# Stick-breaking attention: paired value products, key blocks summed on GpSimd, a reordered TensorE program and a fourth logit buffer

## What is computed

```python
def sb_block(q, k, v, bias, q_pos, k_pos):
    z = jnp.einsum('bqhd,bkhd->bhqk', q, k) * (SB_HEAD_DIM ** -0.5) + bias[None, :, None, None]
    causal = (k_pos[None, :] < q_pos[:, None])[None, None]
    log_stay = jnp.where(causal, jax.nn.log_sigmoid(-z), 0.0)
    between = lax.cumsum(log_stay, axis=3, reverse=True) - log_stay
    weight = jnp.where(causal, jnp.exp(jax.nn.log_sigmoid(z) + between), 0.0)
    return jnp.einsum('bhqk,bkhd->bqhd', weight, v)
```

## Time and profile before

| | us |
|---|---|
| median of 3 runs | 1560.82 |
| lowest and highest run | 1552.71, 1561.26 |
| the profiled execution | 1563.84 |
| its span, first to last instruction | 1561.6 |
| the attention, from the scores of head 0 to the last copy of sample results | 172.64 to 290.52 |

### The profile page before, as it was taken

One profiled execution on the slowest core, in us unless ns is written; L12 is line 12 of the kernel. 1 busy time (PEld: TensorE's weight loads), 2 busy tenths in 40 slices (PEclk: granted clock), 3 DMA queues, 4 the chain that ended last, 5 costly groups with the idle time before them and its releaser, 6 DMA issues. The chain is left out here.

```text
span 1561.6 us, 16192 instructions
## 1 busy us (share of the span) xinstructions
PE 1371.1 (88%) x6197; PEld 1072.5 (69%) x6198; DVE 1038.4 (66%) x1081; ACT 691.2 (44%) x667; POOL 241.2 (15%) x224
## 2 busy tenths in 40 slices
PE   2899899996599989998879999897589999999893
PEld 2786355686478868887758884486568878887672
DVE  3278844214698878885854999523578888886753
ACT  2010344002467867873530007221347777775532
POOL 1033222001112322220000000001102233321000
PEclk6899899996699999999989999998579999999896
DMA  7457536007279999996460302012259999995301
GB/s 268 167 196 302 196 109 241 28 1 264 92 276 371 313 360 373 370 355 234 133 215 1 108 14 99 0 52 59 68 177 372 388 309 382 389 372 221 113 1 55
DMA packets 122739, 314.04 MB, mean 201 GB/s; under 512 B 10060, under 2 KB 10720, under 8 KB 120608
## 3 DMA queue, kind: packets, MB, share of 16 engines
q1 hardware_dynamic: 106350, 249.82, 44.4%
q0 software_dynamic: 14256, 58.69, 10.3%
q10 hardware_dynamic: 2074, 4.71, 1.1%
HBM read 304.17 MB, written 26.70 MB: 212 GB/s over the span
## 5 line engine op out<-in xcount | busy, mean ns | idle before, releaser
L1694 PE MATMUL ps<-xnT,ring 128*128 128x260 f32 x1408 | 318.5, 390 | 13.0 <-DVE xnT L1188 7.0
L1694 PEld LDWEIGHTS ps<-xnT,ring 128*128 128x128 f32 x1408 | 273.2, 194 | 57.9 <-issue 14.4
L1916 PE MATMUL ps<-ring_parts,arena_parts 128*128 128x512 f32 x768 | 308.9, 402 | 0.0
L1448 DVE TENSOR_TENSOR ring_parts<-ring,xnT_parts 128x2048 fp32r<-128x2048 f32 x96 | 219.3, 2291 | 47.8 <-ACT xnT_parts L967 46.8
L1448 DVE TENSOR_TENSOR ring_parts<-ring,arena_parts 128x2048 fp32r<-128x2048 f32 x96 | 219.7, 2291 | 40.2 <-ACT arena_parts L967 39.7
L967 ACT ACTIVATE xnT_parts<-ring 128x2048 fp32r<-128x2048 f32 x96 | 183.4, 1917 | 87.6 <-PE ps L1917 76.4
L967 ACT ACTIVATE arena_parts<-ring 128x2048 fp32r<-128x2048 f32 x96 | 183.5, 1918 | 75.5 <-PE ps L1917 53.1
L1916 PEld LDWEIGHTS ps<-ring_parts,arena_parts 128*128 128x128 f32 x768 | 148.5, 193 | 32.4
L1915 PE MATMUL ps<-xnT_parts,arena_parts 128*128 128x512 f32 x384 | 158.7, 413 | 10.1 <-DVE arena_parts L1452 10.1
L1915 PE MATMUL ps<-arena_parts 128*128 128x512 f32 x384 | 156.4, 407 | 8.4 <-DVE arena_parts L1452 4.7
L1917 PE MATMUL ps<-xnT_parts,arena_parts 128*128 128x512 f32 x384 | 155.1, 404 | 0.0
(11 more groups left out here) (274 smaller groups left out, 1734.6 us busy)
## 6 DMA issues: line engine op xcount, KB each, us to landing
ring<-in_w_gate_e SPq DMA_DIRECT2D x32, 2048.0 KB, 17.5
ring<-in_w_up_e SPq DMA_DIRECT2D x32, 2048.0 KB, 16.7
ring<-in_w_down_e SPq DMA_DIRECT2D x32, 2048.0 KB, 18.4
ring<-in_w_in_ab SPq DMA_DIRECT2D x4, 2048.0 KB, 26.1
ring<-in_w_ple_gate SPq DMA_DIRECT2D x4, 2048.0 KB, 8.1
ring<-y_rows SPq DMA_DIRECT2D x16, 512.0 KB, 7.1
ring<-in_w_in_c SPq DMA_DIRECT2D x4, 2048.0 KB, 8.9
x_rows<-arena ACTq DMA_DIRECT2D x10, 416.0 KB
```

What stands on the lines that cost most here:

```text
L1448: v.tensor_tensor(w_lo, w, high[hu0 % 4].bitcast(F32), ALU.subtract).then_inc(s_lo, 1)
L1694: ins = mm(s[:, half, 0:HALF], w[:, k, :], src[:, k, half * HALF:(half + 1) * HALF], start=(k == 0), stop=(k == n - 1))
L1916: mm(ps[:, bank, :], x, w_lo, start=False, stop=False)
```

## The change

Four things change, all in the attention.

1. GpSimd masks the softplus of head h before the weights of head h-1, no longer after them. It then adds key blocks up into a spare area: two copies of 128 columns, one addition of 128 and one of 384 columns, with two waits on its own results. `sticks` then needs one `ones` product in place of up to three for each key block: seven products, 2048 columns, instead of ten and 2560.
2. `values(p)` takes two heads at a time, key block by key block, and stands in even rounds only, behind the scores of head h+1 and the sample values, and in front of the sticks of head h. It waits for the masked weights of both heads.
3. Sample values and `turn_sample` come one round later; the sample values stand right behind the scores.
4. There are four logit buffers; the fourth lies over queries and keys that have been used by then. Which head takes which, and which value products it waits for, stands in two tuples.

```diff
+LOGIT_BUF = (0, 1, 2, 0, 1, 3, 2, 0)
+LOGIT_FREE = (0, 0, 0, 2, 2, 0, 4, 4)
...
             for h in range(SBH):
+                pool.wait_ge(s_sp, h + 1)
+                sp, later = ex[:, h % 2, :], spare[h % 2]
+                link(mask(sp))
+                pool.tensor_copy(later[:, 0:P], sp[:, 1024:1024 + P])
+                pool.tensor_copy(later[:, 256:256 + P], sp[:, 512:512 + P])
+                link(pool.tensor_tensor(later[:, P:256], sp[:, 1024 + P:1280], sp[:, 896:1024], ALU.add))
+                pool.tensor_tensor(later[:, 256 + P:640], sp[:, 512 + P:896], later[:, 0:256], ALU.add
+                                   ).then_inc(s_spm, 1)
                 if h:
                     mask_weights(h - 1)
-                pool.wait_ge(s_sp, h + 1)
-                mask(ex[:, h % 2, :]).then_inc(s_spm, 1)
...
                 act.wait_ge(s_zf, h + 1)
-                if h >= 3:
-                    act.wait_ge(s_pv, h - 2)
+                if LOGIT_FREE[h]:
+                    act.wait_ge(s_pv, LOGIT_FREE[h])
...
                 if h:
                     pe.wait_ge(s_dd, h)
-                if h >= 2:
-                    turn_sample(h - 2)
+                if h >= 3:
+                    turn_sample(h - 3)
                 pe.wait_ge(s_spm, h + 1)
-                sp = ex[:, h % 2, :]
+                sp, later = ex[:, h % 2, :], spare[h % 2]
+                behind = (later[:, 256:640], later[:, 0:256], sp[:, 896:1024])
                 for kb in range(4):
-                    for src in range(kb, 4):
...
+                    col, width = c0 + at[kb], TP - kb * P
+                    ins = mm(ps_flat[:, col:col + width], tri[:], sp[:, at[kb]:at[kb] + width],
+                             start=True, stop=(kb == 3), skip_group_check=True)
+                    if kb < 3:
+                        ins = mm(ps_flat[:, col + P:col + width], ones[:], behind[kb],
+                                 start=False, stop=True, skip_group_check=True)
                 ins.then_inc(s_cf, 1)
...
+            def values(p):
+                pe.wait_ge(s_wm, 2 * p + 2)
+                if p:
+                    pe.wait_ge(s_ot, p)
                 for kb in range(4):
+                    for h in (2 * p, 2 * p + 1):
+                        rows = slice(64 * (h % 2), 64 * (h % 2) + 64)
+                        ins = mm(ps[rows, 6, kb * P:TP], v_tok[:, kb, h * DH:(h + 1) * DH],
+                                 zs3[LOGIT_BUF[h]][:, at[kb]:at[kb] + TP - kb * P], start=(kb == 0), stop=(kb == 3),
+                                 skip_group_check=True)
+                ins.then_inc(s_pv, 2)
...
             for h in range(SBH):
                 if h + 1 < SBH:
                     scores(h + 1)
-                if h:
-                    values(h - 1)
+                if h >= 2:
+                    sample_values(h - 2)
+                    if h % 2 == 0:
+                        values(h // 2 - 1)
                 sticks(h)
...
+            sample_values(SBH - 2)
+            pe.wait_ge(s_dd, SBH)
+            turn_sample(SBH - 3)
             sample_values(SBH - 1)
-            values(SBH - 1)
-            pe.wait_ge(s_dd, SBH)
             turn_sample(SBH - 2)
+            values(SBH // 2 - 1)
             turn_sample(SBH - 1)
```

More of the change, by code:

```diff
@@ L247, in decoder_step @@
         ar = Arena()
-        qT = ar(4, T)
-        kT = ar(4, T)
+        qk = ar(4, 2, T)
+        qT, kT = qk[:, :, 0, :], qk[:, :, 1, :]
         v_tok = ar(NRT, 512)
@@ L254, in decoder_step @@
         ex = ar(2, 1280)
-        zs3 = [zs[:, 0, :], zs[:, 1, :], xnT[:, 4:KT, :].rearrange("p k t -> p (k t)")[:, 0:1280]]
+        zs3 = [zs[:, 0, :], zs[:, 1, :], xnT[:, 4:KT, :].rearrange("p k t -> p (k t)")[:, 0:1280],
+               arena[:, 0:1280]]
+        spare = [xnT[:].rearrange("p k t -> p (k t)")[:, 3360:4000], sq[:].rearrange("p a b -> p (a b)")[:, 0:640]]
         ar = Arena(spans)
@@ L714, in mask_weights @@
                 pool.wait_ge(s_we, h + 1)
-                mask(zs3[h % 3]).then_inc(s_wm, 1)
+                mask(zs3[LOGIT_BUF[h]]).then_inc(s_wm, 1)
             for h in range(SBH):
+                pool.wait_ge(s_sp, h + 1)
[6 more added lines that the diff above has]
+                                   ).then_inc(s_spm, 1)
                 if h:
                     mask_weights(h - 1)
-                pool.wait_ge(s_sp, h + 1)
-                mask(ex[:, h % 2, :]).then_inc(s_spm, 1)
                 if h < 2:
@@ L910, in weights @@
                 act.wait_ge(s_dd, h + 1)
-                nc.scalar.activation(zs3[h % 3], zs3[h % 3], ACT.Exp).then_inc(s_we, 1)
+                nc.scalar.activation(zs3[LOGIT_BUF[h]], zs3[LOGIT_BUF[h]], ACT.Exp).then_inc(s_we, 1)
             for h in range(SBH):
-                zb, eb = zs3[h % 3], ex[:, h % 2, :]
+                zb, eb = zs3[LOGIT_BUF[h]], ex[:, h % 2, :]
                 act.wait_ge(s_zf, h + 1)
-                if h >= 3:
-                    act.wait_ge(s_pv, h - 2)
+                if LOGIT_FREE[h]:
+                    act.wait_ge(s_pv, LOGIT_FREE[h])
                 nc.scalar.activation(zb, z, ACT.Identity, bias=sbb[:, h:h + 1], scale=DH ** -0.5).then_inc(s_zs, 1)
@@ L1305, in attend_back @@
             def attend_back(h):
-                zb = zs3[h % 3]
+                zb = zs3[LOGIT_BUF[h]]
                 dve.wait_ge(s_cf, h + 1)
@@ L1797, in sticks @@
-                ins.then_inc(s_cf, 1)
[L1799 to L1803, removed]
-                for kb in range(4):
[L1805 to L1808, removed]
+                    col, width = c0 + at[kb], TP - kb * P
@@ L1841, in _ @@
                        ).then_inc(s_cs, 1)
-                else:
-                    sample_values(h - 1)
+            sample_values(SBH - 2)
+            pe.wait_ge(s_dd, SBH)
+            turn_sample(SBH - 3)
             sample_values(SBH - 1)
-            values(SBH - 1)
-            pe.wait_ge(s_dd, SBH)
             turn_sample(SBH - 2)
+            values(SBH // 2 - 1)
             turn_sample(SBH - 1)
```

## The result

| | before | after |
|---|---|---|
| median of 13 runs each, us | 1554.39 | 1542.61 |
| lowest and highest run | 1548.19, 1561.26 | 1535.19, 1549.3 |
| ratio of times, 95% interval | | 0.9921 [0.9899, 0.9943] |
| span of the profiled execution | 1561.6 | 1538.3 |
| the attention stage, as in front | 117.88 (172.64 to 290.52) | 105.29 (171.09 to 276.38) |

The change made the kernel 12 us faster, 0.8%. That is within the 1% that the forecast called no change, but the time, 1542.61, lies 3.4 us under the low end of the range. Two things went into the miss. The 13 runs of the kernel before have a median 6.4 us lower than the three of them that the forecast started from. And the gain was 12 us where 7.4 was forecast: 0.9921 measured, 1553.4 / 1560.8 = 0.9953 forecast, just outside the interval. The second alone would have stayed in the range, at 1560.8 - 12.5 = 1548.3.

The account below looks back on a forecast made before the run. TensorE was taken to set the pace in the attention's middle rounds, not the first ones or round 7. A walked gain of 12.5 us less 5.1 for the clock gave 7.4: 1560.8 to 1553.4 us, range 1546 to 1562.

Parts of the forecast that it names:

- the 1% that the forecast called no change: Whole kernel: 15.6 us counted as indistinguishable; chances 0.85 within 1%, 0.10 faster, 0.05 slower.
- The walk: Attention stage: new order followed instruction by instruction with the old trace's durations; 12.5 us gained before any clock loss.
- the clock term: TensorE idling ahead of three pairs of values: half clock behind each, 3 x 1.7 = 5.1 us lost, ends 0 and 6.6.
- twice the select's 0.83 on 0.185: GpSimd's additions before sticks: twice a select's rate per column, 0.82 us for 384 columns and 0.40 for 128.
- nothing ahead of sticks 2 comes later than before: Start of attention: softplus of head 2 still ends at 204.49, so sticks 2 start at 211.0, 3.6 us gained.
- the clock stays full: Rival, attention: TensorE's stalls cost no clock, so 12.5 us gained, 1548.3 us; chance 0.17.
- both old stalls: Earlier trace, TensorE ahead of values: stalls of 2.14 and 3.06 us, followed by losses of 1.7 and 2.2 us.
- The ceiling: Attention: TensorE's shorter sticks and paired values would give 16 us, 1.0%, if TensorE stayed the pace.
- the 2.27 of the rival: Rival, values: the two heads' products don't run side by side, 2.27 us more four times, 1562.5 us; chance 0.05.
- GpSimd was not late: Rival, ahead of three pairs: dear additions or waits for VectorE, some 2 us a pair, 1559.4 us; chance 0.13.
- Half clock up to the end of the next sticks: Rival, three pairs: values, turned sample and sticks, 6.85 us, take twice that, 8 us slower, 1568.9 us; chance 0.08.
- round 7 (7.1 us): Last attention round: values go behind, leaving 6.4 us of 13.46 between sticks 6 and sticks 7 ends; 7.1 us gained.

Follow-up runs that it names:

- sticks first: Changed kernel with pairs of values behind the sticks of their round and four logit buffers in turn; 1538.19 us (0.9874) and 1535.92 us (0.9877).
- the filled one: Changed kernel with four logit buffers in turn, plus four unneeded products ahead of each of the first three pairs of values; 1543.18 us (0.9913).
- the one with heads in blocks: Changed kernel with a pair's value products issued all for the first head, then all for the second, not alternating; 1547.52 us (0.9936).
- The fourth buffer: Changed kernel with the four logit buffers taken in turn, so head 3 need not wait for the first pair; 1541.58 us (0.9922) and 1535.36 us.
- The triple mask: Changed kernel with GpSimd's mask of the weights run three times instead of once, same data; 1558.12 us (1.0034).
- The first last-round edit: Kernel before with values of head 6 moved behind sticks of head 7, in round 7 alone; 1557.52 us (1.0021).
- the second 1.7 less: Kernel before with values of head 6 behind sticks 7 and GpSimd masking the softplus before the previous head's weights; 1558.04 us, one run.

## Why the prediction was right or wrong

**The walk held.** Starts of sticks in us from the start of the stage, without the clock term. The walked ones come from the prediction's 211.0 for sticks 2 and its durations from there on, less 172.64:

| | walked | measured |
|---|---|---|
| sticks 2 | 38.4 | 38.7 |
| sticks 4 | 62.8 | 62.8 |
| sticks 6 | 85.2 | 84.8 |
| sticks 7 | 91.6 | 91.2 |
| last copy | 105.4 | 105.3 |

12.5 us were walked and 12.6 measured. Its prices were close. Sticks took 3.65 us (3.61 taken), a pair 2.37 (2.33, for which the prediction gives no working; the rate of the earlier trace rows alone would make it 1.94 x 2560 / 2048 = 2.43). GpSimd's sums took 1.8 us, from 227.83 to 229.65 (2.0 taken, bounds 1.6 and 2.5). The difference is in the 384-column addition, 0.73 us where 0.82 was taken, and in the two waits, 0.07 and 0.08 (0.16 each). The form of the addition's price was wrong: from 0.45 us for 128 columns and 0.73 for 384 it is 1.1 ns a column on some 0.31 us, not twice the select's 0.83 on 0.185. The two errors cancel at these sizes, which is luck.

The walk took it that nothing ahead of sticks 2 comes later than before, and there it was 0.6 us off: the softplus of head 2 ended 32.5 us behind the stage's start, 31.9 before. In round 0 VectorE's seven additions ran beside GpSimd's new sums and took 2.53 us instead of 1.83 (the kernel before first, then the change); without the sums they took 1.83 again. The faster sums made up for a third of it.

```profile
185.74 1.83 DVE L1276 TENSOR_TENSOR arena<-arena 128x64 f32<-128x64 f32 x7
184.17 2.53 DVE L1286 TENSOR_TENSOR arena<-arena 128x64 f32<-128x64 f32 x7
```

Of the other kernels, the first with sticks first and the filled one came within 0.3 us of their walks, and the one without sums within 1. The one with heads in blocks came within 0.5 by luck: 2.3 us a pair were expected at full clock, and it paid 1.55 a pair and the rest in half clock. The others missed. The fourth buffer took 3.4 and 1.7 us more than walked and the second execution of sticks first 1.9, each with half clock on the chain. The triple mask took 9.0 more, by the lock with VectorE and by half clock. The first last-round edit took 1.9 more (115.8 expected, 117.72 measured), because its walk left GpSimd's order out, and the second 1.7 less.

**The clock term failed.** "I take 3 x 1.7 = 5.1" is the step. It made one stall of 2.14 us a price for every stall of that length. In three profiles of the change none of nine stalls ahead of values, six of 1.06 to 1.61 us and three of 2.18 to 2.21, was followed by half clock. The rival "the clock stays full" is what happened behind these stalls: 12.5 us, a ratio of 1548.3 / 1560.8 = 0.9920, against 0.9921 measured. I gave it 0.17 because "both old stalls" spoke against it. The experiments show what that evidence was worth. Of the stalls ahead of values in all profiles, the kernel before among them, all eight of 2.74 us and more lost the clock. Of ten between 2.14 and 2.41 us three did and seven did not. Length alone does not decide: the shorter stalls ahead of sticks 1, 1.80 to 1.95 us in the three profiles of the change, were all followed by half clock. The prediction kept 0 as an end of the clock term, but put its weight on the other side. The stalls were also shorter than it said (1.06 us instead of 3.0, 2.18 instead of 2.6). Most of the first difference is the half-clock stretch in sticks 3, which took up 1.7 us of that stall.

**The starting point.** The forecast went down from 1560.8, and 13 runs put the kernel before at 1554.39. With that and the walk alone, 1554.4 - 12.5 = 1541.9, 0.7 us under the time measured, closer than the interval (some 3.4 us either way) can tell. The range allowed for full clock and for a median 3 us off; the median was 6.4 off, and that took the time below the range.

**The ceiling and the other rivals.** TensorE spared 16 us of work was named as a ceiling only, and that is right: without the sums the stage loses 3.3 us, not 7.2. The products do run side by side; in blocks a pair takes 1.55 us more, not the 2.27 of the rival. GpSimd was not late ahead of the three pairs: its masks there took 1.02 or 1.03 us, and no addition was dear. Beside VectorE it was slowed in round 0 alone, where its mask took 1.43 us as in the earlier trace rows. Half clock up to the end of the next sticks did not happen in the change, but once it came near with the buffers in turn (0.67, then 0.59), and cost 3.4 us, not 6.85.

**Where the gain sits.** In the walk round 7 (7.1 us) is the largest part. The two moves that make it, done alone in the kernel before, gave 5.3 us, some 2.2 of it in round 1 and through the clock. So round 7's part is not shown apart from the rest. It is shown that moving the values alone does not do it: with GpSimd's order left, the stall moves on to sticks 7. GpSimd's order alone was not run.

**What stays open.** Why one stall of 2.2 us is followed by half clock and another is not; what each of the four parts of the change gives by itself, since only the sums, the turn of the products and the buffers were varied one at a time; and whether the shorter stage of sticks first makes the whole kernel faster, given that the later stages' clock falls at other moments each time.

## What to carry to other kernels

Walk a new order instruction by instruction with the durations of the trace, including what the helper engine does first; it came out within 0.4 us at each of five points. A clock loss behind a stall seen once is a chance, not a price: keep it as a range around the walk. Filling the stall kept the clock in the one execution here, and other ready work put in front took the stalls ahead of the pairs away. Take the starting time from as many runs as there are, since three can lie 6 us off.

## What the hardware showed that was not expected

A stretch at half clock costs only what lies on the chain: in the change 1.7 us of it were absorbed in full by a wait behind them. The same idle time, 2.18 and 2.19 us, was followed by values of 2.4, 3.44 and 4.03 us, the first in the same execution as each of the others. And products of 64 columns to alternating halves take 2.38 us where the same products in two blocks take 3.93, so the order of issue alone is worth 40%. GpSimd and VectorE slowed each other both ways: 12 selects took 4.56 us instead of 3.21 beside VectorE's pass, and seven additions of VectorE 2.53 instead of 1.83 beside GpSimd's sums.
